# The low half of a shared weight tile, divided at three quarters between VectorE and GpSimd

## The reference

```python
def expert(acc, ew):
    wg, wu, wd, cw = ew
    hid = jax.nn.silu(t @ wg) * (t @ wu)
    return acc + (cw[:, None] * (hid @ wd)).astype(acc.dtype), None
...
def swiglu(h, w_gate_up, w_down):
    g, u = jnp.split(h @ w_gate_up, 2, axis=-1)
    return (jax.nn.silu(g) * u) @ w_down
```

## Time and profile before

| | |
|---|---|
| runs | 2779.74 (median), 2766.6, 2788.76 us |
| profiled execution, first to last instruction | 2783.9 us |
| PE busy | 2328.6 us (84%) |
| DVE busy | 1625.2 us (58%) |
| ACT busy | 1104.4 us (40%) |
| POOL busy | 1323.9 us (48%) |
| stretches with expert slices | 520 to 710 us and 1060 to 1260 us |
| mean granted clock of TensorE in the stretches 520 to 710 and 1060 to 1260 us | 0.99 and 0.99 |

### The profile page before, as it was taken

How to read it: one execution, slowest core, us unless ns; L and a number is a source line. 1 busy time by engine, 2 the same in 40 slices (tenths; PEclk the granted TensorE clock), 3 DMA queues, 4 the chain that set the end, 5 groups by cost and what they waited for, 6 DMA issues and landing times.

```text
span 2783.9 us, 41385 instructions
## 1 busy us (share of the span) xinstructions
PE 2328.6 (84%) x15250; PEld 1960.5 (70%) x15250; DVE 1625.2 (58%) x2522; ACT 1104.4 (40%) x1581; POOL 1323.9 (48%) x744
## 2 busy tenths in 40 slices
PE   5998777788498767785999997768999799999998
PEld 2864545677385466674868995325899699887998
DVE  3488464477558545674247555996555755523654
ACT  3222533466433435764434442001443344444443
POOL 2320132588442336882654552874565256441553
PEclk7995888899797888997989998668999899999999
DMA  5258602699326037883405441001455244342442
GB/s 228 91 202 322 217 15 91 228 341 344 144 96 252 1 112 268 321 296 133 171 24 199 186 172 71 0 0 52 165 192 189 91 181 182 135 152 91 152 181 91
DMA packets 93047, 443.73 MB, mean 159 GB/s; under 512 B 9088, under 2 KB 25600, under 8 KB 56704
## 3 DMA queue, kind: packets, MB, share of 16 engines
q1 hardware_dynamic: 79104, 390.10, 38.6%
q0 software_dynamic: 8496, 31.99, 3.0%
q10 hardware_dynamic: 5328, 20.04, 1.8%
HBM read 401.20 MB, written 40.89 MB: 159 GB/s over the span
## 4 chain that ended last, share of the span: by engine, by line
PE 40%; DVE 5%; POOL 3%; ACT 2%; DVEq 2%; POOLq 1%; issue 1%; DMA 0%; ACTq 0%
PE bank L657 11%; PE bank L658 11%; PE bank L659 11%; POOL ring_halves L371 2%; PE bank L699 2%; ACT high L1212 1%; PE bank L1123 1%; POOLq L593 1%; DVEq L2179 1%; PE bank L1061 1%; DVE HT L1633 1%; POOLq L598 1%; PE bank L1038 1%; DVE rstd L1618 1%; PE bank L1051 1%
## 5 line engine op out<-in xcount | busy, mean ns | idle before, releaser
L371 POOL TENSOR_TENSOR ring_halves<-ring,high 128x1024 fp32r<-128x1024 f32 (+1 forms) x230 | 814.2, 3541 | 953.9 <-ACT high L1212 953.9
L657 PE MATMUL bank<-ssdb_halves,high 128*128 128x256 f32 (+1 forms) x2080 | 619.6, 298 | 65.8 <-DVE HT_halves L1627 34.8
L658 PE MATMUL bank<-HT_halves,high 128*128 128x256 f32 (+1 forms) x2096 | 627.4, 299 | 0.0
L659 PE MATMUL bank<-ssdb_halves,ring_halves 128*128 128x256 f32 (+1 forms) x2080 | 615.5, 296 | 0.0
L1212 ACT CAST high<-ring 128x2048 fp32r<-128x2048 f32 x230 | 438.0, 1906 | 89.7 <-PE bank L659 89.7
L657 PEld LDWEIGHTS bank<-ssdb_halves,high 128*128 128x128 f32 x2080 | 400.8, 193 | 90.5 <-issue 61.2
L371 DVE TENSOR_TENSOR ring_halves<-ring,high 128x1024 fp32r<-128x1024 f32 x200 | 279.5, 1398 | 248.0 <-ACT high L1212 247.9
L658 PEld LDWEIGHTS bank<-HT_halves,high 128*128 128x128 f32 x2096 | 402.6, 192 | 8.9
L659 PEld LDWEIGHTS bank<-ssdb_halves,ring_halves 128*128 128x128 f32 x2080 | 398.4, 192 | 9.6
L378 DVE TENSOR_TENSOR dring_halves<-dring,dhigh 128x512 fp32r<-128x512 f32 x152 | 309.6, 2037 | 53.1 <-ACT dhigh L1218 53.0
L378 POOL TENSOR_TENSOR dring_halves<-dring,dhigh 128x512 fp32r<-128x512 f32 x152 | 264.5, 1740 | 80.7 <-ACT dhigh L1218 80.6
(11 more groups left out here) (415 smaller groups left out, 4603.3 us busy)
## 6 DMA issues: line engine op xcount, KB each, us to landing
ring<-in_ffn SPq DMA_DIRECT2D x88, 1024.0 KB, 5.4
ring<-in_moe SPq DMA_DIRECT2D x64, 1024.0 KB, 7.3
ring<-in_ada SPq DMA_DIRECT2D x48, 1024.0 KB, 6.9
dring<-in_ffn_down SPq DMA_DIRECT2D x88, 512.0 KB, 3.6
dring<-in_moe_down SPq DMA_DIRECT2D x64, 512.0 KB, 4.6
ring<-in_foxin SPq DMA_DIRECT2D x24, 1024.0 KB, 4.8
ring<-in_win SPq DMA_DIRECT2D x22, 1024.0 KB, 4.8
zs_b<-x_slots POOLq DMA_DIRECT2D x32, 512.0 KB, 8.8
```

The costliest lines, as they stand in the source:

```text
L371: eng.tensor_tensor(low, w, h, ALU.subtract).then_inc(sem(f"low_{engine}"), 1)
L657: mm(o, a[0], b[0], start=first, stop=last and bool(kw), **kw)
L658: mm(o, a[0], b[1], start=False, stop=last and bool(kw), **kw)
L659: return mm(o, a[1], b[0], start=False, stop=last, **kw)
```

## The change

One number in `make_low` changes. For a shared tile DVE made columns 0 to 1023 and POOL 1024 to 2047; now DVE makes columns 0 to 1535 and POOL 1536 to 2047. Tiles that are not shared, the order of all instructions, the semaphores and the down tiles stay.

```diff
@@ -363,7 +363,7 @@
 
             if engine == "dve" and not shared(c):
                 return
-            cut = TILE // 2 if shared(c) else 0
+            cut = 3 * TILE // 4 if shared(c) else 0
             at_ = slice(0, cut) if engine == "dve" else slice(cut, TILE)
             w, h = ring[SPLIT[c] % RING][:, at_], high[c % HIGH][:, at_]
             eng.wait_ge(sem("high"), c + 1 + RING * g)
```

## The result

The change made the kernel **27 us slower**: a median of 2811.49 us over 10 runs (2803.12 to 2820.29) against 2781.53 us for the kernel before in the same sessions (10 runs), a ratio of 1.0098 with a 95% interval of 1.0071 to 1.0125, which is 20 to 35 us. (The two medians by themselves are 30 us apart; both figures lie in the interval, and the text goes by the ratio.) The forecast was 2810 us and +30.

A forecast was written before the change was run, and what follows sets the result against it. PE was busiest (84%), with DVE's L371 on every block's path. Experts' 34 us less 3.5 elsewhere gave +30 on the profiled 2783.9, so 2814; that execution lay 4 us above the median, hence 2810 us, range 2780 to 2826.

The forecast's parts named there:

- What bounds it, and the prices: DVE's L371 is on the path of every block; 1536 columns take 1.77 us, POOL's 512 end 1.14 us later.
- Steps 1 to 5: One expert block replayed from DVE's even L371: the odd down projection starts at 7.83 us, where it was 6.70.
- Step 3: In an expert block POOL issues L378 at 2.88 us, ahead of DVE at 3.08, where DVE led by 0.9.
- The count of 30 blocks: Expert blocks that pay, taken from 30 PE waits for L1980: 30 x 1.13 = 34 us.
- Step 6: From the odd down projection to the next block's L371: 5.65 us without slack, so the block is 1.13 us longer.
- The clock: Rival (4%): in the expert stretches PE's new idleness lowers its clock, adding about 30 us: 2840 us.
- the term of 34: Expert slices: 30 blocks, each 1.13 us longer, make the kernel 34 us slower.
- Elsewhere: Outside the experts PE's waits for POOL's L371 go or shrink: -3.5 us, bounds 0 and -4; feed-forward slices 0.
- DVE keeps its place: Rival (13%): in expert blocks DVE stays ahead with L378; +0.13 us a block, +4 us in all, less 3.5: 2780.
- The shorter pair pays: Rival (8%): PE's waits for POOL's part of shared tiles go, L1980 costs nothing more, kernel gets faster: 2765 us.

The follow-up runs named there:

- 11/16: Kernel before, with DVE making eleven sixteenths of the columns of all shared tiles: 2769.79 us, ratio 0.9968.
- 23/32: Kernel before, with DVE making twenty-three thirty-seconds of the columns of all shared tiles: 2816.72 us, ratio 1.0109.
- the five blocks: Blocks with a small delay in a run of the change plus a drain and memset on POOL between even slices' L371 and L378; whole run 2813.2 us.
- the others alone: Kernel before, with three quarters to DVE only in shared tiles outside the expert slices, which stay at one half: 2768.36 us, ratio 0.9957.
- the experts alone: Kernel before, with three quarters to DVE only in tiles of the expert slices, other shared tiles at one half: 2823.82 us, ratio 1.0154.
- 15/16: Kernel before, with DVE making fifteen sixteenths of the columns of all shared tiles: 2812.36 us, ratio 1.0103.

## Why the prediction was right, and where its sum was off

**What bounds it, and the prices.** Right: DVE's L371 is on the path of every block. 1536 columns took 1.76 us (taken: 1.77), and POOL's 512 ended 1.16 us after DVE's (1.14).

**Steps 1 to 5.** Counted from 538.83, with the forecast in brackets: DVE's L371 ends at 1.76 (1.77), the even down projection starts at 2.10 (2.11), POOL's L371 ends at 2.92 (2.91), POOL's L378 is issued at 2.88 (2.88) and DVE's at 3.07 (3.08), which ends at 4.73 (4.71), POOL's odd L371 ends at 5.88 (5.85), DVE's at 7.50 (7.47), and the odd down projection starts at 7.84 (7.83). Step 3 is the one that decides. The 11/16 and 23/32 kernels show it by itself: the jump comes where the lead changes hands, with 64 columns between them. So do the five blocks in which POOL's L378 alone came later. As to what hung on the Trainium skill (SBUF — State Buffer, Who interferes with whom): DVE's L378 took 0.68 us with a lead of 0.07 and 1.78 without, so one instruction waits for the whole of the other, and nothing was served in turns.

The count of 30 blocks is right by luck. The 30 waits of the earlier trace rows are 28 in such blocks and two of 0.77 us in the last blocks, which have no L371; the first block of each layer had no wait. There are 30 blocks with a pair of L371 all the same. (Outside the experts stand 136 shared tiles, not 134.)

**Step 6** was short by 0.08 us. Up to the odd down projection the block is 1.14 longer; from there to the next block's L371 it is 0.07 longer, since PE restarts after a wait where it ran on before. The first four blocks of the first layer, at full clock, took 13.12, 13.26, 13.35 and 13.59 us against 11.90, 12.05, 12.13 and 12.39: 1.20 to 1.22 each. 30 x 1.21 = 36.3 us.

**The clock** was put down as a rival at 4%, not as a term. It took part: the blocks at half clock after the even wait took 13.49 and 13.73 us against 12.10 and 12.35, so 0.17 more than the 1.21. With 14 of them that is 2.4 us, and 36.3 + 2.4 = 38.7, where +38.9 was measured. So the term of 34 should have been 39. In the 23/32 kernel the clock stayed and the loss was the same size, with 0.13 us more of chain.

**"Elsewhere", -3.5 with bounds 0 and -4, was mis-sized.** The change gave 11 back outside the experts in its span, and the others alone gave 12 (6 to 17) in time. The step priced PE's waits for POOL's L371, and those went as forecast: from 1265 on they fell from 4.0 us to 0.4. What it left out is DVE's other instructions that read SBUF while POOL's L371 runs. It had the row of one, L1722, and did not look for more. The kernel before (line, engine, op, out<-in, count: ns least/median/longest, first and last start us; and PE's wait for ACT's L1242, which waits for L2270):

```profile
L2270 DVE SCALAR_TENSOR_TENSOR XT<-XT,vec,rstd x8: 471/472/2637, 1290.7 to 1297.7; 128x256 f32<-128x256 f32 x8
...
PE bank L699 <- ACT wide L1242: 32.6, 12, 8.2
...
L1722 DVE TENSOR_SCALAR wide<-wide x2: 2103/2110/2117, 1315.6 to 2419.9; 128x32 f32<-128x32 f32 x2
...
L2163 DVE TENSOR_TENSOR dring<-con,vec x1: 3360/3360/3360, 1711.8 to 1711.8; 128x1024 f32<-128x1024 f32 x1
```

and the changed one:

```profile
L2270 DVE SCALAR_TENSOR_TENSOR XT<-XT,vec,rstd x8: 473/474/1553, 1332.7 to 1337.6; 128x256 f32<-128x256 f32 x8
...
PE bank L699 <- ACT wide L1242: 29.5, 12, 5.0
...
L1722 DVE TENSOR_SCALAR wide<-wide x2: 1006/1006/1007, 1354.5 to 2448.9; 128x32 f32<-128x32 f32 x2
...
L2163 DVE TENSOR_TENSOR dring<-con,vec x1: 2283/2283/2283, 1742.3 to 1742.3; 128x1024 f32<-128x1024 f32 x1
```

Each held-up instruction lost 1.1 us, as POOL's L371 is 1.1 us shorter; the eight L2270, two of which are held up, go from 7.0 to 4.9 us between first and last start. The two single-site kernels bear out the cause: L2270's longest stays at 2633 ns with the experts alone, and is 1557 with the others alone; L1722 is 2.11 and 1.01 us, L2163 3.36 and 2.29. The Trainium skill (SBUF — State Buffer, Who interferes with whom) says that a DVE instruction with two inputs in SBUF contends with a GpSimd one that reads it, which L2270 and L2163 bear out; read that way, it would have told which rows to look up. PE's own waits tell how much of this lies on the path: the longest for ACT's L1242, which comes from L2270, falls from 8.2 to 5.0 us, and the one for L2163 from 6.5 to 5.9. With the 3.6 us of POOL's L371 (4.0 to 0.4) that is 7.4 us, inside the 6 to 17. All three fall by as much with the others alone, and the first two not at all with the experts alone. What the rest of the 12 is stays open; what is outside the stretches differs by over 13 us between single profiled executions of kernels that make 3/4 or 15/16 there (-2.9 to -16.4 us against before), so one trace cannot tell.

**The sum.** +39 and -12 in place of +34 and -3.5. Two errors of opposite sign made the time come out within 2 us of the forecast. That closeness is luck; taken one by one, each site was missed by 5 to 8 us.

**The rivals.** "DVE keeps its place" did not come, but it is what the 11/16 kernel is: 183.7 us in the first stretch against 184.0. At 3/4 it is what the five blocks with a late L378 on POOL are: 0.24 to 0.29 us longer than before in the two compared, where the rival had 0.13. "The shorter pair pays" is wrong for the experts and right for all other tiles: there little that PE waits for is queued directly behind DVE's L371. L2163 is, and it starts 0.53 us later after the start of L371 than before, but takes 1.08 less; that is why PE's wait for it falls by 0.6 only. The Trainium skill (GPSIMD Engine Reference, Key points) says that DVE is structurally about twice as fast for elementwise work, and the 0.69 us against 1.27 for 512 columns agree. That holds at both sites alike; what differs between them is the queue.

## What to carry to other kernels

Before columns are moved between two engines that hold each other up, replay one block on both queues and note who issues first at each pair of instructions: here a lead of less than 0.1 us decided over a whole instruction, and moving the work a little less far brought a gain without the flip. Judge such work site by site: where the queue behind the faster engine feeds the bottleneck, stop short of the flip; where it feeds nothing, more columns can go. And when an instruction that holds up another engine gets shorter, list every instruction of that engine that takes far more than its usual time, not just those that the bottleneck names. When an experiment misses what it was meant to do, look for the single blocks in which it did it.

## What the runs showed of the hardware

- Six kernels with PE idle for 1.8 to 2.2 us once in a block (the change, the experts alone, 15/16, the two with another order on DVE, and the one with a drain on POOL) showed the granted clock at 0.50 in the stretch behind it in some of the blocks (stretches of experts at 0.90 to 0.98 as a whole), while the 23/32 kernel, with waits of 1.7 and 1.2 us in nearly every block, kept 1.00. Blocks with the same idle time were found at either level, so the idle time alone does not tell which one it will be.
- A product of the down projection that starts after a wait is followed 0.31 us later by the next, and 0.24 us without a wait, both at full clock.
- A drain on POOL behind a 512-column instruction was followed by 0.15 to 4.24 us in which POOL did nothing, most often about 3. It was shortest, 0.15 us, in the last two blocks of each layer, in which POOL issues no load of later rows; whether it is these loads that a drain waits for was not tested.
- An instruction of 32 columns on DVE took 2.11 us behind POOL's L371 of 1024 columns, and 1.01 us behind one of 512.
- POOL's L378 was issued 0.03 us before the row of its L371 ends and, with a lead of 0.05 us over DVE's at 23/32, went first; with DVE ahead by 0.07 us at 11/16, DVE did. Both held in all 30 blocks.
